# Weight slots of a two-block transformer kernel, shifted by multiples of 64 bytes

## The reference

```python
# first block
h = _layer_norm(ALPHA * h + 0.5 * _swiglu(h, ffn1_w_gate, ffn1_w_up, ffn1_w_down), ln1_g, ln1_b)
mix = _token_mixers(h, w_in, ...)             # proj = h @ w_in ... @ w_out
h = _layer_norm(ALPHA * h + mix, ln2_g, ln2_b)
xa = _memory_cross_attention(h, mem, ...)     # wq, wk, wv, wo
h = _layer_norm(ALPHA * h + xa, ln3_g, ln3_b)
h = _layer_norm(ALPHA * h + 0.5 * _swiglu(h, ffn2_w_gate, ffn2_w_up, ffn2_w_down), ln4_g, ln4_b)
# second block
x = x + concatenate([attention, pooling]) @ w_out_2     # both from rmsnorm(x) @ w_in_2
h = rmsnorm(x, norm2_g)
x = x + (silu(h @ w_gate) * (h @ w_up)) @ w_down

def _swiglu(x, w_gate, w_up, w_down):
    return (jax.nn.silu(x @ w_gate) * (x @ w_up)) @ w_down
```

## Time and profile before

| | |
|---|---|
| median of 3 runs | 1666.03 us (1665.79 to 1666.12) |
| span of the profiled execution, first to last instruction | 1663.7 us |
| the median less this span | 2.3 us |
| TensorE busy | 1653.9 us (99%), 8375 matmuls |
| GpSimd, VectorE, ScalarE busy | 704.5, 629.7, 597.6 us |
| DMA queue of the weights, share of 16 engines | 32.8% |

### The profile page before, as it was taken

One profiled execution on the slowest core, in us unless ns is written; L12 is line 12 of the kernel. 1 busy time (PEld: TensorE's weight loads), 2 busy tenths in 40 slices (PEclk: granted clock), 3 DMA queues, 4 the chain that ended last, 5 costly groups with the idle time before them and its releaser, 6 DMA issues.

```text
span 1663.7 us, 20763 instructions
## 1 busy us (share of the span) xinstructions
PE 1653.9 (99%) x8375; PEld 1393.3 (84%) x8375; DVE 629.7 (38%) x1059; ACT 597.6 (36%) x911; POOL 704.5 (42%) x392
## 2 busy tenths in 40 slices
PE   9999999999999999999999999999999999999999
PEld 7888888899888888889888888898768988888888
DVE  4111121257565777656121111257763512121122
ACT  4122222247545555436221222247574322122220
POOL 4454444554572443133454444444323444344442
PEclk9999999999999999999999999999999999999999
DMA  7333243333222444123333243351113333323332
GB/s 208 91 102 92 83 117 89 101 104 111 77 64 64 127 129 144 57 77 89 91 99 101 74 117 99 92 156 42 44 32 80 86 101 93 97 83 110 99 89 77
DMA packets 296041, 157.58 MB, mean 95 GB/s; under 512 B 5265, under 2 KB 292618, under 8 KB 295946
## 3 DMA queue, kind: packets, MB, share of 16 engines
q1 hardware_dynamic: 295946, 156.26, 32.8%
HBM read 154.14 MB, written 2.10 MB: 94 GB/s over the span
## 4 chain that ended last, share of the span: by engine, by line
PE 93%; DVE 3%; ACT 2%; issue 1%; DMA 1%; POOL 0%; SPq 0%; DVEq 0%; POOLq 0%
PE bank L551 22%; PE bank L552 22%; PE bank L555 22%; PE bank L2349 2%; PE bank L2353 2%; PE bank L2350 2%; PE bank L594 2%; PE bank L595 2%; PE bank L599 2%; PE bank L2846 2%; PE bank L574 1%; PE bank L580 1%; PE bank L575 1%; PE bank L2834 1%; PE bank L2375 1%; PE bank L2594 1%
## 5 line engine op out<-in xcount | busy, mean ns | idle before, releaser
L479 POOL TENSOR_TENSOR wlo<-wraw,whi 128x1024 fp32r<-128x1024 f32 (+1 forms) x238 | 561.4, 2372 | 771.3 <-ACT whi L474 771.3
L551 PE MATMUL bank<-ahi,whi 128*128 128x512 f32 x1294 | 507.8, 392 | 0.0
L552 PE MATMUL bank<-alo,whi 128*128 128x512 f32 x1294 | 503.8, 389 | 0.0
L474 ACT CAST whi<-wraw 128x1024 fp32r<-128x1024 f32 (+1 forms) x268 | 268.0, 1025 | 232.6 <-PE bank L555 152.9
L555 PE MATMUL bank<-ahi,wlo 128*128 128x512 f32 x1294 | 320.9, 389 | 0.0
L551 PEld LDWEIGHTS bank<-ahi,whi 128*128 128x128 f32 x1294 | 243.0, 188 | 51.4 <-issue 1.2
L552 PEld LDWEIGHTS bank<-alo,whi 128*128 128x128 f32 x1294 | 242.9, 188 | 51.2 <-issue 1.4
L555 PEld LDWEIGHTS bank<-ahi,wlo 128*128 128x128 f32 x1294 | 242.9, 188 | 50.4
L1649 DVE SCALAR_TENSOR_TENSOR hval<-gate,bank 128x512 f32<-128x512 f32 x66 | 45.4, 687 | 554.4 <-PE bank L555 540.2
L1044 ACT ACTIVATE gate<-bank 128x512 f32<-128x512 f32 x66 | 39.5, 598 | 512.8 <-PE bank L555 500.6
L1658 DVE SCALAR_TENSOR_TENSOR res<-res,bank 128x512 f32<-128x512 f32 x78 | 52.7, 685 | 236.3 <-PE bank L555 163.8
(11 more groups left out here) (380 smaller groups left out, 2285.0 us busy)
## 6 DMA issues: line engine op xcount, KB each, us to landing
wraw<-in_ffn_w_gate SPq DMA_DIRECT2D x42, 512.0 KB, 3.9
wraw<-in_ffn_w_up SPq DMA_DIRECT2D x42, 512.0 KB, 3.9
wraw<-in_ffn_w_down SPq DMA_DIRECT2D x32, 512.0 KB, 3.6
wraw<-in_w_in SPq DMA_DIRECT2D x30, 512.0 KB, 4.0
wraw<-in_w_gate SPq DMA_DIRECT2D x21, 512.0 KB, 3.9
wraw<-in_w_up SPq DMA_DIRECT2D x21, 512.0 KB, 3.9
wraw<-in_w_out SPq DMA_DIRECT2D x16, 512.0 KB, 5.2
wraw<-in_w_down SPq DMA_DIRECT2D x16, 512.0 KB, 3.7
```

The costliest lines, as they stand in the source:

```text
L474: eng.copy(high_of(b)[:, 0:n], raw_of(b)[:, 0:n]).then_inc(hi_ready, 1)
L479: eng.tensor_tensor(low_of(b)[:, 0:n], raw_of(b)[:, 0:n], high_of(b)[:, 0:n], ALU.subtract).then_inc(LO[b][0], 1)
L551: eng.matmul(o, w, xhi[:, k, :], start=(k == 0), stop=False)
L552: eng.matmul(o, w, xlo[:, k, :], start=False, stop=False)
```

## The change

Each of the six raw slots (in which the lo part lies too) and each of the four hi slots gets a start of its own, in words of 4 bytes: 16, 32, 48, 64, 96, 112 for raw slots 0 to 5 (64 to 448 bytes), and 0, 48, 64, 80 for hi slots 0 to 3 (0 to 320 bytes). Blocks in `NARROW` stay at 16 words, the last two blocks at 0. The address holds for the load, both splits and the matmuls. And `multiply_tokens` takes the slots of the last two blocks from `HI_AT` and `RAW_AT`: hi slots 0 and 1 as before, lo slots 0 and 1, where their lo parts are, in place of 2 and 3.

```diff
+        RAW_SKEW = (16, 32, 48, 64, 96, 112)
+        HI_SKEW = (0, 48, 64, 80)
+
-        def slot(ring, b, n):
+        def slot(ring, b, n, skews):
 
-            at = SKEW if any(first <= b < end for first, end in NARROW) else 0
+            at = SKEW if any(first <= b < end for first, end in NARROW) else 0 if b >= len(blocks) - 2 else skews[n]
             return ring[:, n, at:at + KD * P]
 
         def raw_of(b):
-            return early_raw[:, EARLY_RAW[b][0], :] if b in EARLY_RAW else slot(wraw, b, RAW_AT[b] % RAW)
+            return early_raw[:, EARLY_RAW[b][0], :] if b in EARLY_RAW else slot(wraw, b, RAW_AT[b] % RAW, RAW_SKEW)
 
         def low_of(b):
-            return early_lo[:, EARLY_RAW[b][0], :] if b in EARLY_RAW else slot(wlo, b, RAW_AT[b] % RAW)
+            return early_lo[:, EARLY_RAW[b][0], :] if b in EARLY_RAW else slot(wlo, b, RAW_AT[b] % RAW, RAW_SKEW)
 
         def high_of(b):
-            return early_hi[:, EARLY_HI[b], :] if b in EARLY_HI else slot(whi, b, HI_AT[b] % 4)
+            return early_hi[:, EARLY_HI[b], :] if b in EARLY_HI else slot(whi, b, HI_AT[b] % 4, HI_SKEW)
...
             def multiply_tokens(ph):
                 b = ph.base + LAST
-                at = b % 4, b % RAW
+                at = HI_AT[b] % 4, RAW_AT[b] % RAW
```

## The result

The changed kernel takes 1681.57 us (median of 4 runs, 1681.28 to 1681.85) against 1665.91 us before: 15.7 us more, a ratio of 1.0098 with a 95% interval of 1.0084 to 1.0112. It is slower, by about 1%. The profiled execution has a span of 1679.1 us, 15.4 more than before, at a granted clock of 1.000.

A forecast was written before the change was run, and what follows sets the result against it. TensorE's matmul pace was taken to bound the kernel. Shifts, splits and loads, and the last two blocks each counted 0, leaving the median of before: 1666.0 us, likeliest case 1663 to 1669, whole range 1645 to 1684 us.

The forecast's parts named there:

- What bounds the kernel: Whole kernel: TensorE, busy 99% of the span; weight buffers matter only through its matmul pace or a late split or load.
- one nanosecond on each of them is 5.4 us: Full-width matmuls reading ring slots: 5400 records at 226.7 ns, 1224 us, nearly three quarters of the span.
- Splits and loads: GpSimd splits and weight loads at shifted addresses: covered whether faster or slower, so 0 us.
- The last two blocks: End of the kernel, lo slots 0 and 1 read instead of 2 and 3: cost 0, at most 2.4 us.
- The shifts: Full-width ring blocks: 4500 matmuls get a new weight address; taken as 0, bounds 53 us less and 19 us more.
- I take nothing, from two rows: Full-width shifts at 0 us: the stream settles from 232 to 226.7 ns, and half width also takes 17 cycles per 16 columns.
- what went before decides, not the weight's address: Half-width matmuls at 64 bytes: same block, weights and slots run at 113.3 or 117.5 ns in the two token halves.
- the 19 us: Upward bound for the shifted full-width matmuls: 4.2 ns, the gap between two half-width paces, on 4500.
- a worse settled pace: Slower rival, all shifted full-width matmuls: 4.2 ns each, 19 us more, 1685 us; chance 0.07.
- four forms: Full-width ring-slot matmuls: four grouped instructions, each standing for three alike (hi by hi, hi by lo, lo by hi), 5400 records.
- unsettled passages: Slower rival, full-width ring blocks: 488 offset jumps between hi and lo weights at 26.5 ns, 13 us, 1679 us; chance 0.13.
- the 17th cycle is a collision: Faster rival: equal weight and operand offsets cost 6.7 ns per matmul; shifting 4500 saves 30 us, 1636 us; chance 0.20.

## Why the prediction was wrong

*What bounds the kernel* was right: TensorE's pace alone moved the end, and "one nanosecond on each of them is 5.4 us" sized what came. *Splits and loads* at nothing: right. GpSimd's splits keep their median of 2.4 us, beside the earlier trace rows:

```profile
L482 POOL TENSOR_TENSOR wlo<-wraw,whi x238: 1835/2405/2928, 21.0 to 1652.4; 128x1024 fp32r<-128x1024 f32 x107, 128x768 fp32r<-128x768 f32 x12
```

*The last two blocks* at nothing: right, by the run of that part alone.

*The shifts* at nothing: wrong, and this is the step that failed, where the prediction says "I take nothing, from two rows". Its own sign of being wrong, a pace that moves by 0.7 ns or more, came true with 3.2 ns. Both readings were of a kernel with one offset. From the settling to 226.7 ns I concluded that two streams find a phase without collision, whatever the address. But they settle to a pace that belongs to the offset: other offsets settle too, to 229.0 or 233.3 ns. And from 17 cycles per 16 columns at both widths I concluded that the cost is the operand stream's own. That the ratios agree is a coincidence of the two offsets in use, 0 at full width and 64 at half width: at 64 bytes full width has 560 cycles for 512 columns, at 0 half width has 288 for 256. That argument also misread the weight load: at half width it does not fill "nearly the whole matmul", its record is longer than the 113.3 ns between two starts:

```profile
L2349 PEld LDWEIGHTS bank<-hid,whi 128*128 128x128 f32 x128 | 24.1, 188 | 0.1
```

The sentence "what went before decides, not the weight's address" was true of the one offset that the rows had; at 0 and at 192 bytes, the timelines shown have one pace in both token halves.

The measured time lies inside the whole range of 1645 to 1684 us, but that is no credit to the forecast: 1663 to 1669 was the range of its case, and the upper end stood there for rivals that were priced otherwise. Of the bounds, the 19 us held for this mixture of offsets only; its 4.2 ns per matmul did not, since 64 bytes cost 6.6 ns, and all slots at 64 bytes 33 us. The rival with the right mechanism was "a worse settled pace", to which I gave 0.07 at 1685 us. Its price was 4.2 ns on 4500 matmuls; measured are 3.2 ns on each full-width spacing (mean 226.9 before, 230.1 after, over the 4884 of `multiply`, without those above 300 ns); on 5472 that is 17.3 us, or 3.8 ns on each of 4500. (The prediction's four forms leave out 120 of the 5520 matmuls that read ring slots at full width, my 5472 the 48 of the first two blocks.) The two spans differ by 15.4 us because `mk` takes 2.0 us less: 1.4 are the stretch at half the clock, which only the execution before has, and 0.6 are its third to last blocks, which go at 113.3 ns where they went at 117.8. The rival "unsettled passages" came nearest to the time (1679 us) with the wrong mechanism, by luck: without any jump the loss doubles (1698 us). Its sign, spacings of 230 to 236 ns behind a first read of lo weights, could not tell it from a worse pace: after the change they appear, but at 64 bytes 231 and 236 alternate to the last matmul of the stretch. From the paces of the offsets alone, the six lo slots lie 6.6, 5.8, 2.3, 0, 5.8 and about 4.2 ns above 226.7 (448 bytes, between its two paces), 4.1 on average, and the four hi slots 0, 2.3, 0 and 6.6, 2.2 on average: 1824 x 4.1 + 3648 x 2.2 ns = 15.5 us, so by this estimate some 2 us of the 17.3 are left for the passages.

The rival "the 17th cycle is a collision" was right on half width (0 bytes: 120 ns with contiguous columns too) and wrong to carry it over: equal offsets are the best case at full width. Two half-width stages flipped, one each way: `mk` as said, and the stage at 1124 us, where most went from 113.3 to 117.8 ns, 0.5 us more.

The Trainium skill, "TensorE: Matmul & The Clock Gate", Part 2, gives the weight load a read port of its own that takes nothing from the running matmul. The runs here do not agree: with the streamed operand where it was, a shift of the weights by 64 bytes makes a matmul 6.6 ns longer. They show that the two reads are not independent, and not how.

What stays open: where in the chip the two reads meet, and why 192 bytes show two paces. No run streamed operands without a weight load beside them, so whether 226.7 ns is the stream's own floor isn't shown; none of the offsets run went below it.

## What to carry to other kernels

Where TensorE streams one-pass 32-bit operands and loads new weights for each matmul, as in this kernel, try the weights' start at a multiple of 256 bytes from the streamed operand's for 512 columns, and measure the offset anew for 256 columns: the best one at full width was the worst one at half width. A pace that is the same everywhere in a trace does not say that it can't depend on a thing that is also the same everywhere; bound it by a run with one value changed, not by an argument from ratios. When buffers get offsets for one engine's sake, check the pace of the engine that bounds the kernel first. And before a difference of 2 us is read from two executions, compare their granted clocks.

## What the runs showed of the hardware that I had not expected

- Full-width matmuls by the weights' offset from the streamed operand, modulo 256 bytes: 0, 226.7 ns; 192, 229.0 (or 233); 128, 232.5 in a pattern of seven; 64, 233.3; off the grid of 64 bytes 16, 233.0, 96, 234.3, and 32, 48, 160 and 224 near 233.3. That it counts modulo 256 rests on 0 and 256, 64 and 320, 128 and 384, 192 and 448.
- Half-width matmuls: 64 bytes, 113.3 or 117.8 ns (the same stage went at one before the change and at the other after it, with its offset untouched); 192, 117.8; 32, 118.3; 96, 117.3 to 120; 128, 118.7 or 120; 0, 120.
- It is the difference of the two addresses that counts: all buffers 64 bytes on cost nothing (1665.71 us).
- Three of thirteen traces have 3.4 us at a granted clock of 0.50 in `mk`; in the one of before, 256 columns took 213 ns there, and 113 to 118 at 1.00.
